# Three more expert blocks in three fp32r passes beside the key search, their low parts made by GpSimd

## The reference, cut to what matters

```python
q = (xt @ w_query).reshape(T, H, 2, PEER_HALF)
s = jnp.einsum('thcd,cnd->thcn', q, sub_keys)
sv, si = lax.top_k(s, K)                                   # K = 16, 8 heads, two key halves
cand_s = (sv[:, :, 0, :, None] + sv[:, :, 1, None, :]).reshape(T, H, K * K)
top_s, pos = lax.top_k(cand_s, K)
idx = jnp.take_along_axis(cand_i, pos, axis=-1)
gate = jax.nn.softmax(top_s, axis=-1)
a = jnp.einsum('thkd,td->thk', down[ib], xb)
c = gb * jax.nn.gelu(a)
out = jnp.einsum('thk,thkd->td', c, up[ib])
```

## Time and profile before

| what | value |
|---|---|
| median of 3 runs | 2825.68 us (2825.58 to 2825.96) |
| the profiled execution: its own time | 2825.48 us |
| its span, first to last instruction | 2823.7 us |
| PE busy | 2803.2 us, 99% of the span |
| DVE busy | 1943.8 us, 69% |
| ACT busy | 1419.7 us, 50% |
| POOL busy | 148.4 us, 5% |

### The profile page before, as it was taken

The page is one execution under the profiler, slowest core; times in us unless marked ns, Lnnn a source line. Parts: engine busy times, 40 slices in busy tenths (PEclk is TensorE's granted clock), DMA queues, the critical chain, the costliest instruction groups (busy, mean ns, idle before and its releaser), DMA issues.

```text
span 2823.7 us, 45734 instructions
## 1 busy us (share of the span) xinstructions
PE 2803.2 (99%) x18566; PEld 2528.1 (90%) x18566; DVE 1943.8 (69%) x2882; ACT 1419.7 (50%) x1707; POOL 148.4 (5%) x145
## 2 busy tenths in 40 slices
PE   8999999999999999999999999999999999999998
PEld 7899998899999889999889999988899988888997
DVE  7889888655555788988865555576656556565664
ACT  6653554544444665355454444455455444545543
POOL 0033110000000003311000000000000000000000
PEclk9999999999999999999999999999999999999999
DMA  6344666855553534466685555465555656554663
GB/s 214 124 162 138 218 247 208 287 213 199 186 194 141 187 120 158 141 217 239 205 288 215 194 192 193 149 223 170 181 166 182 187 188 185 171 180 155 175 187 133
DMA packets 219570, 530.21 MB, mean 188 GB/s; under 512 B 13546, under 2 KB 87440, under 8 KB 208400
## 3 DMA queue, kind: packets, MB, share of 16 engines
q1 hardware_dynamic: 212944, 504.32, 54.2%
q0 software_dynamic: 6464, 23.61, 2.1%
HBM read 507.81 MB, written 20.06 MB: 187 GB/s over the span
## 4 chain that ended last, share of the span: by engine, by line
PE 98%; DVE 1%; DMA 1%; issue 0%; ACT 0%; SPq 0%; DVEq 0%
PE ps L2666 17%; PE ps L2648 13%; PE ps L1537 13%; PE ps L1547 12%; PE ps L1525 12%; PE ps L1480 11%; PE ps L607 4%; PE ps L598 4%; PE ps L1451 2%; PE ps L2925 2%; PE ps L1462 1%; PE ps L1255 1%; PE ps L2834 0%; PE ps L2818 0%; DMA ring<-in_peer_down 0%; PE ps L1367 0%
## 5 line engine op out<-in xcount | busy, mean ns | idle before, releaser
L2267 DVE TENSOR_TENSOR ring_lo<-ring,w_hi 128x1024 fp32r<-128x1024 f32 x320 | 388.2, 1224 | 243.0 <-ACT w_hi L2263 241.7
L2263 ACT ACTIVATE w_hi<-ring 128x1024 fp32r<-128x1024 f32 x320 | 335.2, 1056 | 236.1 <-PE ps L2666 169.0
L1537 PE MATMUL ps<-h_t_lo,down_hi 128*128 128x256 f32 x1024 | 288.2, 281 | 0.0
L1537 PE MATMUL ps<-h_t_expert,down_lo 128*128 128x256 f32 x1024 | 287.8, 281 | 0.0
L1537 PE MATMUL ps<-h_t_expert,down_hi 128*128 128x256 f32 x1024 | 286.8, 280 | 0.0
L2648 PE MATMUL ps<-h_t_lo,w_hi 128*128 128x256 f32 x928 | 260.7, 281 | 0.0
L2648 PE MATMUL ps<-h_t_hi,w_hi 128*128 128x256 f32 x928 | 259.4, 280 | 0.1
L2648 PE MATMUL ps<-h_t_hi,ring_lo 128*128 128x256 f32 x928 | 259.0, 279 | 0.0
L1143 ACT ACTIVATE out_hi<-ring 128x1024 fp32r<-128x1024 f32 x128 | 135.7, 1060 | 162.0 <-PE ps L1525 154.6
L2030 DVE TENSOR_TENSOR up_lo<-ring,up_hi 128x2048 fp32r<-128x2048 f32 x64 | 146.7, 2292 | 97.7 <-ACT up_hi L1134 97.7
L2023 DVE TENSOR_TENSOR out_lo<-ring,out_hi 128x1024 fp32r<-128x1024 f32 x128 | 156.6, 1224 | 77.1 <-ACT out_hi L1143 77.1
(11 more groups left out here) (532 smaller groups left out, 7403.5 us busy)
## 6 DMA issues: line engine op xcount, KB each, us to landing
ring<-in_peer_down SPq DMA_DIRECT2D x128, 1024.0 KB, 5.6
ring<-in_w_in SPq DMA_DIRECT2D x140, 512.0 KB, 3.7
ring<-in_peer_up SPq DMA_DIRECT2D x66, 1024.0 KB, 4.8
ring<-in_w SPq DMA_DIRECT2D x132, 512.0 KB, 3.8
ring<-in_peer_up SPq DMA_DIRECT2D x124, 512.0 KB, 4.2
late_gates<-arena POOLq DMA_DIRECT2D x64, 256.0 KB, 5.2
arena<-late_gates SPq DMA_DIRECT2D x16, 1024.0 KB, 6.4
ring<-in_w_out SPq DMA_DIRECT2D x16, 512.0 KB, 4.1
```

The source lines that it names most:

```text
L1537: m = pe.e.matmul(PS[:, 4 + b, j * T:(j + 1) * T], w[:, b, o], x[:, kc, :], start=kc == 0 and n == 0, stop=kc == KD - 1 and n == 2)
L2263: a.e.activation(W_HI[:, g % HI_SLOTS, :], RAW[:, g % RAW_SLOTS, :], ACT.Copy).then_inc(*a.count(f"c{g}_hi"))
L2267: v.e.tensor_tensor(RAW_LO[:, g % RAW_SLOTS, :], RAW[:, g % RAW_SLOTS, :], W_HI[:, g % HI_SLOTS, :].bitcast(F32), ALU.subtract).then_inc(* ...
```

## The change

`LEAD_SPLIT` gets blocks 4, 7 and 11, which used the fp32 matmuls, so that all of 1 to 13 go through the three passes. The four lists of `LOWS` grow from 7, 3, 7 and 3 halves to 9, 4, 9 and 4, in the order of the blocks. `act_quarter` goes, and with it a wait of DVE's `HT_LO` for the last fp32 block.

```diff
-LEAD_SPLIT = [1, 2, 3, 5, 6, 8, 9, 10, 12, 13]
+LEAD_SPLIT = list(range(1, LEAD))
-LOWS = {"sort_keys0": ((1, 0), (1, 1), (2, 0), (2, 1), (3, 0), (3, 1), (5, 0)), "sort_pairs0": ((5, 1), (6, 0), (6, 1)),
-        "sort_keys1": ((8, 0), (8, 1), (9, 0), (9, 1), (10, 0), (10, 1), (12, 0)), "sort_pairs1": ((12, 1), (13, 0), (13, 1))}
+_HALVES = [(b, j) for b in LEAD_SPLIT for j in range(2)]
+LOWS = {"sort_keys0": _HALVES[0:9], "sort_pairs0": _HALVES[9:13], "sort_keys1": _HALVES[13:22], "sort_pairs1": _HALVES[22:]}
...
-            def act_quarter(b, q):
-
-                if q == 0:
-                    pe.e.wait_ge(*pe.at(f"down_in{b}"))
-                    pe.e.wait_ge(*pe.at("key_ev0" if b < 2 else f"act_ev{b - 2}"))
-                j, first = divmod(q, 2)
-                for kc in range(4 * first, 4 * first + 4):
-                    m = pe.e.matmul(PS[:, act_bank(b), j * T:(j + 1) * T],
-                                    lead_raw(b, j, RAW)[:, kc * P:(kc + 1) * P], HT[:, kc, :],
-                                    start=kc == 0, stop=kc == KD - 1)
-                if q == 3:
-                    m.then_inc(*pe.count(f"act_mm{b}"))
-
...
             def act_part(b, q):
 
-                if b == 0 or b in LEAD_SPLIT or b in GATE_SPLIT or b >= FIRST_TURN:
-                    if b == OWN_X and q == 0:
-                        pe.e.wait_ge(*pe.at("ht_lo"))
-                    passes_quarter(b, q)
-                else:
-                    act_quarter(b, q)
+                if b == OWN_X and q == 0:
+                    pe.e.wait_ge(*pe.at("ht_lo"))
+                passes_quarter(b, q)
...
             v.e.wait_ge(*v.at("ht_hi"))
-            v.e.wait_ge(*v.at(f"act_mm{max(b for b in range(1, LEAD) if b not in LEAD_SPLIT)}"))
```

## The result

The changed kernel is slower: 2842.7 us (median of 4 runs, 2841.39 to 2844.86) against 2825.6 for the kernel before, a ratio of 1.0061 (95% interval 1.0044 to 1.0078), or 17.1 us more. The forecast was 9.4 us more and a range up to 2840.0: the direction and the first half of the loss are as forecast, the size is not. Because `act_quarter` is gone, the lines that the rows name have moved up: L1480 is now L1467, L1506 is L1490, L2101 is L2085, L2122 is L2106, L2125 is L2109, L2145 and L2146 are L2129 and L2130, L2213 is L2197, and L2221 is L2204.

The account below looks back on a forecast made before the run. PE, busy 99% of the span, bounds the kernel, with DVE almost as full. Holds of DVE outweigh PE's 3.6 us gain a layer, so block 14 starts 4.7 us later, 9.4 us in both: 2835.1 us, range 2828.0 to 2840.0.

Parts of the forecast that it names:

- the hold: DVE beside POOL: a small DVE instruction waits until POOL's instruction ends, 2.2 us each, taken for two-input TENSOR_TENSORs too.
- steps 2, 3 and 5: First layer's DVE marks: pairs at 211.5, second keys at 229.3, the one after the second key sorting at 253.7.
- PE's wait at (7, 1): Block 7's second half: PE wants its low part at 227.7, POOL has it at 231.9, so PE waits 4.2 us.
- Only one-tensor instructions are held: Rival on DVE's hold: TENSOR_TENSORs go unhindered, block 14 starts 1.6 us later a layer, 2828.7 us; 18 in 100.
- Behind this nothing is won back: After block 14, started 4.7 us late: PE bounds the rest and DVE's next work shifts alike, 9.4 us over both layers.
- The gain stays: Rival: DVE is held no longer than now, hkr stays at 264.54, block 14 starts 3.2 us earlier, 2819.1 us; 10 in 100.
- the first one's loss is hidden, since PE then waits less at the second: PE's waits at (7, 1) and block 14: a slow restart after the first adds nothing to the layer's time.
- step 6: First layer's last list: POOL's four halves end at 263.3, L2145 is held until then, hkr ends at 272.6.
- PE comes back slower after its waits: Rival: cold restarts cost 1 to 2 us for each second wait, giving 2837 to 2839 us; 15 in 100.
- Step 7: Block 14's start: its first low half comes 1.2 us behind hkr, 273.8 against 269.02, put at 4.7 us later.

Follow-up runs that it names:

- e3: Kernel before, no block added, with idle GpSimd subtractions ahead of the last half of each list: 2834.7 us, ratio 1.0031.
- e1: Changed kernel without the low parts of blocks 4, 7 and 11, whose third pass rereads the high part: 2824.0 us, ratio 0.9992.
- e8: Changed kernel without low parts of blocks 4, 7 and 11, and with (15, 1)'s low part moved ahead of DVE's key reads: 2818.9 us, ratio 0.9975.
- e2: Changed kernel with idle fp32 matmuls on PE in its two long waits, ahead of block 7's second half and of hkr: 2840.6 us, ratio 1.0052.
- e9: Changed kernel with idle matmuls in PE's two long waits and (15, 1)'s low part moved ahead of DVE's key reads: 2838.1 us, ratio 1.0042.
- e11: Changed kernel with nine idle fp32 matmuls ahead of block 7's second half only, none in the wait for hkr: 2843.0 us, ratio 1.0061.
- e12: Changed kernel with (15, 1)'s low part moved ahead of DVE's key reads, no idle matmuls: 2842.9 us, ratio 1.0061.

## Why the prediction was right or wrong

**Right: the hold, its size and its kind.** L2106 and two of the four L2109 are held to the ends of POOL's halves, the marks are within 0.5 us of steps 2, 3 and 5 in the first layer and of 2 and 3 in the second, PE's wait at (7, 1) is 4.0 us (forecast 4.2). The rival *Only one-tensor instructions are held* fell with one row, 5.33 us for L2109. The Trainium skill ("SBUF — State Buffer", section "Who interferes with whom") says that a VectorE instruction with two inputs in SBUF contends with a GpSimd instruction that reads SBUF. The trace agrees, with those 5.33 us in place of 0.89. e3 shows the same with nothing but POOL's work changed.

**Wrong: "Behind this nothing is won back: PE is what bounds the rest, and DVE's next work ... is shifted with it."** This is the step that failed. I measured DVE's lead at the one place where PE first meets it behind `hkr`, block 14, found 3.3 us, and took it that behind that place both only shift. But DVE works 11.9 us behind `hkr` without a gap until (15, 1), and there its lead was 1.22 us. Once block 14 starts right behind `hkr`, PE arrives at (15, 1) too early: block 14 to the first sum takes 12.2 us and not 10.08, 2.1 us in each layer, 4.2 us in all. e1 and e8 show it without any late `hkr`, and e3 shows that the price of a late `hkr` is set here. The statement of the rival *The gain stays*, that it is decided at a shift of 3.3 us, has the same fault.

**Wrong: "the first one's loss is hidden, since PE then waits less at the second."** The sum put the clock at nothing, and this sentence of a rival is all that it says of the first wait. The half clock behind the wait for (7, 1) costs PE itself something that the second wait would cover. But it also lets PE end block 8 later, and with it the load of block 11 starts later, its high part comes later, and POOL's third list ends later. DVE then meets POOL's halves where the forecast has none: in the first layer it is held at L2129 and at L2130, where step 6 has one hold, and in the second layer the mark of the second pairs is 1.5 us late. Behind its mark `hkr` is 1.4 and 1.9 us later than forecast (89.77 and 90.29 to 88.4), and block 14 is 1.5 and 2.0 us later, 3.5 us in all. In the six layers of e2, e9 and e11, where the first wait is bridged, `hkr` is at 88.28 to 89.35 and POOL waits 0.96 to 1.14 us ahead of (11, 0); in the four of the changed kernel and e12 it is at 89.77 to 90.34, and POOL waits 2.46 to 4.67 us. The means are 1.45 us apart, so most of the 1.7 us a layer is the clock. The loss at the second wait, for which I had priced the rival *PE comes back slower after its waits*, is the one that is hidden: in the first layer e2, at full clock, and the changed kernel have the same 12.2 us to the first sum.

**The sum again.** Step 7's own numbers, 273.8 against 269.02, are 4.8 us and not 4.7, so the steps give 9.6 us. With 3.5 us for the later block 14 and 4.2 for (15, 1) that is 17.3; the rows have 17.35 at the first sum, and the medians 17.1. The profiled execution has 2.2 us more than the median. Its first layer has a PE wait of 2.0 us near 299, for a low part behind a load that took 7.5 us, and a clock of 0.66 to 0.77 up to 306. The other layer has 0.5 us at that place behind a load of 6.0 us. The kernel before has 1.84 us there behind one of 7.3 and 0.48 behind one of 6.0. That part goes by the load of the execution and not by the change.

**What stays open.** Why e11 doesn't show in its median the 2.6 us that its rows have at the first sum (e12's have 0.7 there, which its median can't settle); why the load of block 11 took 7.2 us in one layer; and what moves the first mark by up to 2.7 us between executions of the same instructions.

## What to carry to other kernels

An engine's lead over another has to be taken at every later place where they meet, not at the first one: the smallest is the slack. An engine that runs without gaps behind the event has the same lag to each of them whatever the other one saves. Work handed to an engine that shares its access with the one on the critical chain is free only while it lies beside instructions that are not held; here the sorting was, the short vector operations were not, and the block whose low parts fit in there was worth its full 1.2 us a layer. A wait that is hidden at its own place can still cost through what the waiting engine releases.

## What the runs showed of the hardware that was not expected

The granted clock fell behind all four long waits of the changed kernel (3.4 to 4.0 us; 0.50 at 1163 to 1165 and at 1207 to 1209 in the second layer). It also fell behind some waits of about 2 us and not behind others: in the changed kernel behind the one of 1.98 us near 299 (0.77 over 300 to 303, 0.66 over 303 to 306), in the second layers of e1 and e2 behind the 1.89 us at (15, 1), but not in their first layers behind the same wait, nor in the kernel before behind its 1.84 us. Eight transposes in a cold start had been the only hint before, at a clock shown as 1.00 (which the prediction names for this, are of the 14 blocks; 7 to 9 in that trace shows 1.00 too). Idle fp32 matmuls in the long waits kept it at 1.00 behind them. Beside POOL's subtraction, MAX8 and the other sorting instructions and 128x1 copies ran unhindered in every run; a TENSOR_TENSOR of 128x16, the smallest held here, took 2.38 us in this row of the changed kernel, beside the POOL half that runs from 251.09 to about 253.5 (a third of the row of three halves shown above):

```profile
251.20 2.38 DVE L2123 TENSOR_TENSOR arena<-arena 128x16 uint32<-128x16 uint32 x1
```
